# A DRAM bounce with its two token tiles interleaved: four scattered writes and one plain read instead of one plain write and four gathering reads

## What is computed

```
proj   = rms_norm(x, norm_in_g) @ w_in                       # 2048 -> 15872
mkv    = rms_norm(mem, norm_mem_g) @ w_mem_kv                # 2048 -> 2048
merged = g_a * (ya @ w_proj_a) + g_b * (yb @ w_proj_b) + g_m * (ym @ w_proj_m)
x      = rms_norm(x + merged @ w_out, norm_final_g)
proj2  = rmsnorm(x, ln1_w) @ w_in_2 ;  h = x + y @ w_out_2
ff     = silu(u @ w_ffn_gate) * (u @ w_ffn_up)               # 2048 -> 5632
out    = rmsnorm(h + ff @ w_ffn_down, final_norm_w)
```

## Time and profile before

| | |
|---|---|
| median of 3 runs (lowest, highest) | 2201.22 us (2200.91, 2202.69) |
| profiled execution, its own time | 2200.99 us |
| its span from first to last instruction | 2199.2 us |
| PE, weight loads, DVE, ACT, POOL busy | 99%, 82%, 59%, 47%, 7% of the span |
| DMA | 464.65 MB, mean 211 GB/s |

### The profile page before, as it was taken

One profiled execution on the slowest core, in us unless ns is written; L12 is line 12 of the kernel. 1 busy time (PEld: TensorE's weight loads), 2 busy tenths in 40 slices (PEclk: granted clock), 3 DMA queues, 4 the chain that ended last, 5 costly groups with the idle time before them and its releaser, 6 DMA issues.

```text
span 2199.2 us, 26113 instructions
## 1 busy us (share of the span) xinstructions
PE 2183.5 (99%) x9906; PEld 1810.7 (82%) x9906; DVE 1303.1 (59%) x1559; ACT 1027.7 (47%) x1235; POOL 144.6 (7%) x242
## 2 busy tenths in 40 slices
PE   8999999999999999999999999999999999999998
PEld 7888888888888888888888888888888888888886
DVE  5755656676455645546676888665555555554544
ACT  5544444444444444444555666454444444444443
POOL 0010101011000000000111100110001000100000
PEclk9999999999999999999999999999999999999999
DMA  8775656577754657667778756676777777776664
GB/s 290 220 231 174 204 170 211 183 227 233 211 160 151 213 179 227 202 207 280 231 255 253 227 185 192 199 246 207 216 213 224 216 211 215 229 227 199 194 195 145
DMA packets 228674, 464.65 MB, mean 211 GB/s; under 512 B 16345, under 2 KB 16609, under 8 KB 227681
## 3 DMA queue, kind: packets, MB, share of 16 engines
q1 hardware_dynamic: 212128, 408.73, 59.4%
q0 software_dynamic: 15712, 53.49, 8.0%
q10 hardware_dynamic: 736, 1.12, 0.1%
HBM read 437.59 MB, written 25.69 MB: 211 GB/s over the span
## 4 chain that ended last, share of the span: by engine, by line
PE 95%; DMA 2%; DVE 2%; issue 1%; ACT 1%; POOL 0%; SPq 0%; POOLq 0%; ACTq 0%; DVEq 0%
PE ps L1483 30%; PE ps L1485 30%; PE ps L1484 30%; DMA stage<-bounce 1%; PE ps L1374 1%; PE ps L1396 1%; PE ps L1343 1%; DVE w_lo L864 1%; DMA bounce<-tmp 0%; DMA raw<-in_w_mem_kv 0%; PE ps L1385 0%; ACT w_hi L578 0%; DVE tmp L1025 0%; POOL stage L521 0%; DVE stage L1020 0%
## 5 line engine op out<-in xcount | busy, mean ns | idle before, releaser
L864 DVE TENSOR_TENSOR w_lo<-raw,w_hi 128x1024 fp32r<-128x1024 f32 (+1 forms) x776 | 931.6, 1211 | 765.3 <-ACT w_hi L578 764.2
L578 ACT ACTIVATE w_hi<-raw 128x1024 fp32r<-128x1024 f32 (+1 forms) x776 | 811.6, 1052 | 912.3 <-PE ps L1485 826.0
L1483 PE MATMUL ps<-w_hi,xT_hi 128*128 128x512 f32 x1088 | 430.1, 395 | 0.4 <-DVE w_lo L864 0.4
L1485 PE MATMUL ps<-w_hi,xT_lo 128*128 128x512 f32 x1088 | 424.2, 390 | 0.0
L1484 PE MATMUL ps<-w_lo,xT_hi 128*128 128x512 f32 x1088 | 423.6, 389 | 0.0
L1483 PE MATMUL ps<-w_hi,u2T_hi 128*128 128x512 f32 x704 | 274.0, 389 | 0.0
L1485 PE MATMUL ps<-w_hi,u2T_lo 128*128 128x512 f32 x704 | 273.9, 389 | 0.0
L1484 PE MATMUL ps<-w_lo,u2T_hi 128*128 128x512 f32 x704 | 273.9, 389 | 0.0
L1485 PEld LDWEIGHTS ps<-w_hi,xT_lo 128*128 128x128 f32 x1088 | 204.2, 188 | 43.2
L1483 PEld LDWEIGHTS ps<-w_hi,xT_hi 128*128 128x128 f32 x1088 | 204.4, 188 | 42.5 <-DVE w_lo L864 1.9
L1484 PEld LDWEIGHTS ps<-w_lo,xT_hi 128*128 128x128 f32 x1088 | 204.5, 188 | 41.0
(11 more groups left out here) (262 smaller groups left out, 2250.0 us busy)
## 6 DMA issues: line engine op xcount, KB each, us to landing
raw<-in_w_in SPq DMA_DIRECT2D x368, 512.0 KB, 4.4
raw<-in_w_ffn_gate SPq DMA_DIRECT2D x88, 512.0 KB, 4.3
raw<-in_w_ffn_up SPq DMA_DIRECT2D x88, 512.0 KB, 4.5
raw<-in_w_ffn_down SPq DMA_DIRECT2D x88, 512.0 KB, 4.6
raw<-in_w_out SPq DMA_DIRECT2D x64, 512.0 KB, 5.1
bounce<-tmp POOLq DMA_DIRECT2D x41, 512.0 KB, 3.3
stage<-bounce POOLq DMA_DIRECT2D x164, 128.0 KB, 5.3
raw<-in_w_mem_kv SPq DMA_DIRECT2D x32, 512.0 KB, 5.9
```

The lines of the kernel that those rows point to most:

```text
L578: nc.scalar.activation(w_hi[:, s, 0:per], raw[:, s, 0:per], ACT.Copy).then_inc(hi_ready, 1)
L864: nc.vector.tensor_tensor(w_lo[:, s, 0:per], raw[:, s, 0:per], w_hi[:, s, 0:per].bitcast(F32), ALU.subtract)\
L1483: nc.tensor.matmul(bank(2 * par + t), x_hi, w_hi[:, s, k], start=first, stop=False)
L1485: ins = nc.tensor.matmul(bank(2 * par + t), x_lo, w_hi[:, s, k], start=False, stop=last)
```

## The change

`turn_blocks` writes each token tile's transposed blocks to a place of `tmp` in which both token tiles of the same 32 destination partitions are neighbours (256 floats, 1 KB). The write to `bounce` becomes four DMAs, one for each 32 source partitions, each of 32 x 4 pieces of 1 KB. The read back becomes one DMA of 128 rows of 4 KB. `stage` then holds its data as (q, t, c, b) instead of (t, q, c, b), and every reader of it is adapted: ACT's copies of a whole group are cut in two by token tile, DVE's low parts of "ffu" and "mix" groups go from four instructions of 256 elements to two of 512, and those of "res" groups from four of 256 to eight of 128. A factor 0.5 moves out of these readers into the squared norm factor and into the residual addition.

```diff
-        turned = stage[:, :, :].rearrange("p t (q c b) -> p c (t q) b", c=QUAD, b=32)
+        turned = stage[:, :, :].rearrange("p t n -> p (t n)").rearrange("p (q t c b) -> p c t q b", q=4, t=NT, c=QUAD)
+        blocks_of = tmp[:, :, :].rearrange("p t n -> p (t n)").rearrange("p (m t c b) -> p t m c b", m=4, t=NT, c=QUAD)
...
-                        pool.wait_ge(b_in, 64 * b)
-                    pool.dma_start(bounce, tmp[:, :, :].rearrange("p t n -> p (t n)")).then_inc(b_out, 16)
-                    pool.wait_ge(b_out, 16 * (b + 1))
+                        pool.wait_ge(b_in, 16 * b)
+                    for q in range(4):
+                        pool.dma_start(bounce.rearrange("(m a) (q x) -> q a m x", a=32, q=4)[q],
+                                       tmp[32 * q:32 * (q + 1), :, :].rearrange("p t n -> p (t n)").rearrange("p (m x) -> p m x", m=4))\
+                            .then_inc(b_out, 16)
+                    pool.wait_ge(b_out, 64 * (b + 1))
...
-                    for m in range(4):
-                        pool.dma_start(stage[32 * m:32 * (m + 1), :, :].rearrange("p t (q x) -> p t q x", q=4),
-                                       bounce.rearrange("(q a) (t m x) -> m a t q x", a=32, t=NT, m=4)[m]).then_inc(b_in, 16)
+                    pool.dma_start(stage[:, :, :].rearrange("p t n -> p (t n)"), bounce).then_inc(b_in, 16)
...
-                        nc.scalar.activation(by_block(dst[:, bass.ds(kind[-1] * QUAD, QUAD)]), turned, ACT.Copy, scale=0.5)\
-                          .then_inc(b_hi, 1)
+                        to = by_block(dst[:, bass.ds(kind[-1] * QUAD, QUAD)])
+                        for t in range(NT):
+                            ins = nc.scalar.activation(to[:, :, t], turned[:, :, t], ACT.Copy)
+                        ins.then_inc(b_hi, 1)
...
-                ins = nc.vector.tensor_tensor(f["square"], f["r"], f["r"], ALU.mult)
+                ins = nc.vector.scalar_tensor_tensor(f["square"], f["r"], 0.5, f["r"], ALU.mult, ALU.mult)
...
-                    ins = nc.vector.transpose(tmp[:, t], src(t).rearrange("p (c m a) -> p m c a", c=4, m=4))
+                    ins = nc.vector.transpose(blocks_of[:, t], src(t).rearrange("p (c m a) -> p m c a", c=4, m=4))
...
-                    last = nc.vector.tensor_tensor(dst[:, :, cs], dst[:, :, cs], both(par), ALU.add)
+                    last = nc.vector.scalar_tensor_tensor(dst[:, :, cs], both(par), 0.5 if what == "u" else 1.0, dst[:, :, cs], ALU.mult, ALU.add)
...
-                            ins = nc.vector.scalar_tensor_tensor(lo, turned[:, k], cols[:, f["v"] + kc:f["v"] + kc + 1], hi,
-                                                                 ALU.mult, ALU.subtract)
+                            for t in range(NT):
+                                ins = nc.vector.scalar_tensor_tensor(lo[:, t], turned[:, k, t], cols[:, f["v"] + kc:f["v"] + kc + 1], hi[:, t],
+                                                                     ALU.mult, ALU.subtract)
...
-                        for k in range(QUAD):
-                            ins = nc.vector.scalar_tensor_tensor(lo[:, k], turned[:, k], 0.5, hi[:, k], ALU.mult, ALU.subtract)
+                        for t in range(NT):
+                            ins = nc.vector.tensor_tensor(lo[:, :, t], turned[:, :, t], hi[:, :, t], ALU.subtract)
```

More of the change, by code:

```diff
@@ L707, in post_job @@
                     src = ps[:, 4 * NW:6 * NW].rearrange("p (c s) -> p c s", s=S)
-                    nc.scalar.activation(mrgT_hi[:, bass.ds(kind[-1] * QUAD, QUAD)], src, ACT.Copy, scale=0.5).then_inc(tx_hi[0], 1)
+                    nc.scalar.activation(mrgT_hi[:, bass.ds(kind[-1] * QUAD, QUAD)], src, ACT.Copy).then_inc(tx_hi[0], 1)
                 w.count_job(prev)
@@ L718, in use_late @@
                     kind, _ = late.pop()
-                    act.wait_ge(b_in, w.times("b", 64, 1))
+                    act.wait_ge(b_in, w.times("b", 16, 1))
                     if kind[0] == "res":
@@ L723, in use_late @@
                             kc = kind[2] * QUAD + c
-                            ins = nc.scalar.activation(hi[:, kc].rearrange("p (u b) -> p u b", b=32), turned[:, c], ACT.Copy,
+                            ins = nc.scalar.activation(hi[:, kc].rearrange("p (t q b) -> p t q b", t=NT, b=32), turned[:, c], ACT.Copy,
                                                        scale=cols[:, v + kc:v + kc + 1])
@@ L728, in use_late @@
                         dst = ffT_hi if kind[0] == "ffu" else mrgT_hi
-                        nc.scalar.activation(by_block(dst[:, bass.ds(kind[-1] * QUAD, QUAD)]), turned, ACT.Copy, scale=0.5)\
-                          .then_inc(b_hi, 1)
-                    else:
-                        nc.scalar.activation(by_block(kind[1][:, kind[2]:kind[2] + QUAD]), turned, ACT.Copy).then_inc(b_used, 1)
+                        to = by_block(dst[:, bass.ds(kind[-1] * QUAD, QUAD)])
+                        for t in range(NT):
+                            ins = nc.scalar.activation(to[:, :, t], turned[:, :, t], ACT.Copy)
+                        ins.then_inc(b_hi, 1)
+                    else:
+                        to = by_block(kind[1][:, kind[2]:kind[2] + QUAD])
+                        for t in range(NT):
+                            ins = nc.scalar.activation(to[:, :, t], turned[:, :, t], ACT.Copy)
+                        ins.then_inc(b_used, 1)
                     w.step("b")
@@ L785, in _ @@
                                     6: [mem_in, lambda: squares(mem_tok, sumsq_m, lambda t: None)]}
-            four[1]["act_hooks"] = {7: [lambda: act.wait_ge(b_out, 16),
+            four[1]["act_hooks"] = {7: [lambda: act.wait_ge(b_out, 64),
                                         lambda: squares(x_tok, sumsq_x, lambda t: act.wait_ge(in_x[t], 16 * QUAD))]}
@@ L1137, in use_late @@
                             kc = kind[2] * QUAD + k
-                            lo, hi = (m[:, kc].rearrange("p (u b) -> p u b", b=32) for m in (f["lo"], f["hi"].bitcast(F32)))
-                            ins = nc.vector.scalar_tensor_tensor(lo, turned[:, k], cols[:, f["v"] + kc:f["v"] + kc + 1], hi,
-                                                                 ALU.mult, ALU.subtract)
+                            lo, hi = (m[:, kc].rearrange("p (t q b) -> p t q b", t=NT, b=32) for m in (f["lo"], f["hi"].bitcast(F32)))
+                            for t in range(NT):
+                                ins = nc.vector.scalar_tensor_tensor(lo[:, t], turned[:, k, t], cols[:, f["v"] + kc:f["v"] + kc + 1], hi[:, t],
+                                                                     ALU.mult, ALU.subtract)
                         ins.then_inc(b_used, 1)
```

6 lines of the change are left out of this document (3 added, 3 removed).

## The result

The changed kernel takes 2222.09 us (median of 4 runs, 2220.25 to 2223.95), the kernel before 2201.26 beside it (4 runs, 2200.91 to 2202.69): a ratio of 1.0091, interval 1.0077 to 1.0105. It is 21 us slower, far outside the predicted range. The profiled execution is the one of 2223.95 us.

What follows compares the result with a forecast made beforehand. PE's stream of matmuls was taken to bound the kernel, busy 2183.5 of 2199.2 us. Terms -0.6 + 0.3 + 0.3 = 0.0 us on the profiled 2200.99 us gave 2201.0 us, range 2199.9 to 2203.6.

Steps and rivals of the forecast that it cites:

- The write, 5.7 us by pieces: Write to `bounce`: 512 pieces of 1 KB, interpolated by piece count between 3.3 and 9.0 us, would take 5.7 us.
- The read, 4.1 us: Read back from `bounce`: 128 pieces of 4 KB would take 4.1 us, between 3.3 and 4.4.
- The bounce, 10.1 us for 12.6: Write's issue to last read landing: 5.7 + 0.3 + 4.1 = 10.1 us against 12.6, 2.5 shorter.
- the bounce is as long as before: Rival for the whole bounce: no shortening, since pieces only changed sides; 2201.9 us, chance 0.18.
- Term A: Rope run, 470 to 543 us: a shorter bounce removes PE's waits for `w_lo`; -0.6 us.
- Term B: `res` tiles, 1035 to 1110 us: eight DVE low parts for four delay `w_lo`; +0.3 us, between -0.3 and +0.6.
- Term C: First bounce: a longer write delays ACT's squares of `x_tok` and so PE; +0.3 us, between 0 and 0.75.
- The rest, 0: Everything else, including other DVE low parts, feed-forward, transposes, residual addition and POOL, idle for 93%: 0 us.
- The slow rival: New write as slow as the old reads, bounce 13.7 us: 2205 to 2209 us; 0.06 for over 4.4 us.
- If PE's steps of 0.23 us change anywhere: Sign of being wrong: matmul starts on PE no longer 0.23 us apart, a mechanism the prediction did not have.

Runs made afterwards that it cites:

- the kernel with one DMA of rows: The changed kernel with its write as one DMA of 128 rows of 4 KB, blocks not moved to their partitions; 2201.87 us, ratio 0.9996.
- the control: The changed kernel run once more with nothing altered, on the same chip as a run with added PE transposes; 2217.71 us, ratio 1.0068.
- the version with four reads: The changed kernel, complete, with one write DMA of 512 pieces of 1 KB and four read DMAs of 32 rows; 2202.83 us, ratio 1.0003.

## Why the prediction was wrong

**The step that failed** is the sentence that "the bounce matters only where its lateness eats up all of DVE's lead over PE", and the search that followed from it. I looked for a late bounce where PE already waited, and the chain of waits led to the rope run. But a wait of 0.6 us of PE says nothing of a place with 1 us of slack and none used. The tiles with units were such a place: ACT waited in the first of them for `stage` 0.55 us, which is a sign that the group comes just in time, and ACT's queue behind it holds what PE needs next. The right question to each of the 41 bounces would have been how much later it may land, not how late it is.

**Term by term.**
- *The write, 5.7 us by pieces.* It took 6.8. "It is the pieces that count and not the number of DMAs" is wrong in both halves: rows of 4 KB in four DMAs take 6.4, the 1 KB pieces in one DMA 4.2. I had taken it from `ga_w`, one DMA that took 8.5 us, and from reads, whose cost does not carry over to writes.
- *The read, 4.1 us.* 5.3 on average (median 5.0), and 6.6 to 7.4 in the tiles that decided. The weight loads beside it had been in both of my bounds, but in other stretches.
- *The bounce, 10.1 us for 12.6.* 12.4 on average, before and after. The rival "the bounce is as long as before" held in its condition and not in its price, since the average hid the place: in the tiles with units the reads of before had taken 5.5 to 7.0 us from their issue and not 9.0, so there the new read saved little or nothing, and 10.5 became 13.7.
- *Term A, -0.6 in the rope run.* The mechanism is right: in the kernel with one DMA of rows, bounces of 9.6 us, the wait at 542 us is gone, and PE's stream gains 0.5 us there and 0.2 one round earlier. Its timeline of PE:

```profile
541.51 0.39 PE L1490 MATMUL ps<-w_hi,xT_lo 128*128 128x512 f32 x1
541.74 0.39 PE L1488 MATMUL ps<-w_hi,xT_hi 128*128 128x512 f32 x1
541.96 0.39 PE L1489 MATMUL ps<-w_lo,xT_hi 128*128 128x512 f32 x1
```

  After the change the same wait is gone as well, for -0.3 us; but the chain still leaves PE, at 330 to 385 and 429 to 518 us, now for the tiles with units.
- *Term B, +0.6 on DVE.* The eight low parts take 2.2 us as predicted. Timeline of DVE after, beside the earlier trace rows:

```profile
1078.19 2.19 DVE L1147 SCALAR_TENSOR_TENSOR uT_lo<-stage,cols,uT_hi 128x128 fp32r<-128x128 f32 x8 [0.38 <-ACT uT_hi L726]
```

  In the change PE gains 0.3 us at this place, the best that I had reckoned with. A step of +0.8 stands one tile on, at 1131 us of the kernel after, behind eight more low parts and late weight loads, but the control hasn't got it. In the version with four reads the place cost +1.3.
- *Term C, +0.3 at the first bounce.* 0.0. Timeline of ACT after, beside the earlier trace rows:

```profile
50.20 1.91 ACT L589 ACTIVATE sq_out<-x_tok 128x2048 bf16<-128x2048 f32 x1 [0.18 <-DMA bounce<-tmp]
```

  The write landed 8.1 us after its issue for 7.4, and ACT lost 0.2 us: as I had put it, what slowed this one was not its pieces.
- *The rest, 0.* Right for PE's stream, whose lateness changes by no more than 0.1 us from 1131 us to its end. Not right behind it: POOL's "idle for 93% of the span" hid that its drain is the last thing to end, and 3.2 us come from there.
- *The slow rival* had the right sign and cause (a slow write), but its price was worked out in the rope run, as 2205 to 2209 us. It was to decide "from a bounce of some 14 us"; the places that decided did so from 10.5 to 11.5 us. Its chance of 0.06 for the part over 4.4 us rested on that price.
- "If PE's steps of 0.23 us change anywhere": they did, in the profiled execution and not in the control, and the waits came first.

The Trainium skill (DMA: Bandwidth & Descriptors, section Anatomy of one DMA, SWDGE path) gives one DMA 2.0 us and its bytes over 436e3. For the single write of rows the traces are near it: 512 KB take 3.2 us (median), by an estimate from the page 3.2. The single read of the same size takes 5.0 us (median) beside the weight loads, where the estimate is 3.2 as well. For four writes of 128 KB issued 0.55 us apart, an estimate by that page was 4.0 us, and the runs show 6.4. So here the rule fits the single write, and neither the single read nor four writes behind each other on one queue.

## What to carry to other kernels

An in-order engine that waits a little for a transfer, with work behind it that the busiest engine needs soon, is a deadline: for each use of a transfer, note the slack before PE waits, not only the waits there are. Averages over 41 transfers, or durations from the stretch one has in view, say nothing of the place with the least slack. Splitting a 512 KB write of POOL's queue in four cost 3 us here and four times smaller pieces under one, so a write that shuffles did better here with its shuffle in the pieces of one DMA than in several DMAs; and the span should be split at PE's last matmul before differences of 3 us are explained by the stream.

## What the runs showed of the hardware that I had not expected

- Four writes of 128 KB, issued 0.55 us apart, landed 2.3, 4.5, 5.9 and 6.8 us (medians) after the first one's issue in the trace of the change: nearly behind each other, though all of one DMA lands in 3.2 to 3.9.
- After waits of PE of 1.9 and 3.3 us, one execution shows the granted clock at 0.57 and 0.55 for 4 and 6 us, and another of the same kernel, with waits of 1.4 and 3.6 us at the same places, shows it at 1.00. What makes the difference stays open.
- The drain of POOL's queue at the program's end takes 1.7 to 10.3 us, the same to 0.01 us in both profiled executions of the changed kernel and in those with the same transfers, 0.083 us more for each DMA added, and this although the last of these transfers had landed over 200 us before.
